# Half-width products of a head pair in two groups, and the softmax denominators and row of ones around them, in a two-layer attention kernel

## The reference, cut to what matters

```python
# per family: q, k (768 tokens), v
s = einsum('bqkgd,blkd->bkgql', qblk, k).astype(float32) * scale
p = softmax(s, axis=-1)
o = einsum('bkgql,blkd->bqkgd', p, v)
# latents read all 768 keys; context tokens read the 256 context keys (layer 0 only)
# gqa: 6 heads of 64; diff: 4 x 2 maps of 32, o1 - lam * o2, then rms_norm; mla: 6 heads of 64+32
y = concat(o * silu(g)) @ w_out
x = layer_norm(alpha * x + gate * y)
```

## Time and profile before

| | us |
|---|---|
| three runs, lowest, median, highest | 1100.06, 1102.35, 1105.29 |
| the profiled execution | 1105.77 |
| its span in the trace | 1103.9 |
| attention of layer 0 on PE, first max tile to last turned output | about 265 to 514 |
| attention of layer 1 | about 811 to 1031 |

### The profile page before, as it was taken

The page is one execution under the profiler, slowest core; times in us unless marked ns, Lnnn a source line. Parts: engine busy times, 40 slices in busy tenths (PEclk is TensorE's granted clock), DMA queues, the critical chain, the costliest instruction groups (busy, mean ns, idle before and its releaser), DMA issues.

```text
span 1103.9 us, 13093 instructions
## 1 busy us (share of the span) xinstructions
PE 969.0 (88%) x4607; PEld 684.6 (62%) x4607; DVE 594.0 (54%) x901; ACT 403.4 (37%) x815; POOL 524.8 (48%) x421
## 2 busy tenths in 40 slices
PE   4799999996899899998995299899968999999793
PEld 2478777985554455555784289789755445555572
DVE  5419230244568499824069548341645758782337
ACT  1521122314354466554200333133434445555320
POOL 2227232352557455553345337243626756566464
PEclk9799999996899899999998689899959989899997
DMA  9756451215232100012431022123142130001421
GB/s 364 270 178 218 157 188 40 77 31 125 55 77 65 34 16 8 16 58 79 169 96 77 38 62 72 58 65 85 49 101 65 37 72 16 15 16 58 160 69 77
DMA packets 44976, 96.91 MB, mean 88 GB/s; under 512 B 9592, under 2 KB 16656, under 8 KB 42864
## 3 DMA queue, kind: packets, MB, share of 16 engines
q1 hardware_dynamic: 43472, 90.83, 26.8%
q10 hardware_dynamic: 1440, 5.24, 1.2%
HBM read 71.33 MB, written 5.26 MB: 69 GB/s over the span
## 4 chain that ended last, share of the span: by engine, by line
PE 71%; DVE 10%; POOL 4%; ACT 4%; SPq 4%; DMA 3%; issue 3%; POOLq 0%; ACTq 0%; DVEq 0%
PE banks L762 13%; PE banks L764 12%; PE banks L763 12%; PE banks L936 11%; PE banks L956 9%; PE banks L914 5%; SPq L588 3%; PE banks L773 2%; DMA area_g<-in_w_ada_dram 2%; DVE negmax L1635 1%; PE banks L975 1%; DVE stats L1515 1%; DVE area_b L1779 1%; PE banks L968 1%; PE banks L826 1%
## 5 line engine op out<-in xcount | busy, mean ns | idle before, releaser
L1393 POOL TENSOR_TENSOR w_split<-w_raw,w_split 128x512 fp32r<-128x512 f32 (+4 forms) x124 | 146.2, 1184 | 258.7 <-ACT w_split L1138 258.6
L762 PE MATMUL banks<-w_split,area_a 128*128 128x512 f32 (+3 forms) x624 | 232.7, 373 | 16.4 <-DVE area_a L1845 9.9
L764 PE MATMUL banks<-w_split,area_a 128*128 128x512 f32 (+3 forms) x624 | 229.8, 368 | 0.0
L763 PE MATMUL banks<-w_split,area_a 128*128 128x512 f32 (+3 forms) x624 | 229.7, 368 | 0.0
L1635 DVE TENSOR_REDUCE negmax<-banks 128x1 f32<-128x768 f32 x160 | 149.6, 951 | 67.3 <-PE banks L914 66.4
L1138 ACT ACTIVATE w_split<-w_raw 128x512 fp32r<-128x512 f32 (+4 forms) x124 | 69.9, 581 | 278.1 <-PE banks L764 278.1
L936 PE MATMUL banks<-area_a 97*128 97x512 f32 (+4 forms) x448 | 135.7, 416 | 17.5 <-DMA area_a<-m_row 11.5
L762 PEld LDWEIGHTS banks<-w_split,area_a 128*128 128x128 f32 x624 | 119.4, 191 | 46.2 <-issue 16.4
L1237 ACT ACTIVATE area_z<-banks 128x512 f32<-128x512 f32 x196 | 109.1, 595 | 103.5 <-PE banks L936 98.2
L764 PEld LDWEIGHTS banks<-w_split,area_a 128*128 128x128 f32 x624 | 118.9, 190 | 16.6
L763 PEld LDWEIGHTS banks<-w_split,area_a 128*128 128x128 f32 x624 | 119.2, 191 | 15.5
(11 more groups left out here) (184 smaller groups left out, 1458.4 us busy)
## 6 DMA issues: line engine op xcount, KB each, us to landing
area_g<-in_w_ada_dram SPq DMA_DIRECT2D x16, 1024.0 KB, 5.8
w_raw<-in_w_in_dram SPq DMA_DIRECT2D x32, 512.0 KB, 3.7
area_g<-in_w_ada_dram SPq DMA_DIRECT2D x16, 512.0 KB, 5.0
w_raw<-in_w_out_dram SPq DMA_DIRECT2D x16, 512.0 KB, 3.9
area_a<-parts SPq DMA_DIRECT2D x72, 96.0 KB
area_a<-parts SPq DMA_DIRECT2D x30, 192.0 KB, 3.6
area_b<-in_x_dram SPq DMA_DIRECT2D x8, 512.0 KB, 9.8
x_mid<-area_b ACTq DMA_DIRECT2D x6, 512.0 KB, 2.7
```

The costliest lines, as they stand in the source:

```text
L762: nc.tensor.matmul(dst, a[0], b[0], start=first, stop=False)
L763: nc.tensor.matmul(dst, a[0], b[1], start=False, stop=False)
L764: return nc.tensor.matmul(dst, a[1], b[0], start=False, stop=last)
L1393: op = nc.gpsimd.tensor_tensor(lo, raw, hi.bitcast(F32), ALU.subtract)
```

## The change

The order of an attention layer is rewritten; the arithmetic stays.

- The step "ctx" comes first in a pair and not last, and its denominators are computed within the pair. The latent denominators of pair p-1 and the context ones of pair p share one bank and one copy.
- The mixes of a pair stand in two groups. After the scores of steps ctx, 0 and 1 come the last two mixes of the pair before (4 and 5), the context mix, the denominators, and mixes 0 and 1, with nothing between; after the scores of 2 and 3 come mixes 2 and 3 and the turned denominators.
- The maximum tiles are dealt out by a table, `max_counts`: how many stand at each of eleven places of a pair. c[3] is the place right ahead of the first group, c[4] the one behind it.
- The rows of ones are written once per layer into all eight blocks by eight DMAs (`load_ones`), behind the max row of pair 1; a diff unit then has six DMAs and not seven. SP loads unit 12 and 13 one pair later (the list with 12, 13 and 14 at p = 4), behind the max row of pair 4.
- `mla_high` of a pair's first head moves from the next pair to the end of its own, and ACT's copy of the latents stands ahead of the exponentials of step 1. On DVE `output_rows` comes after five to seven of the pair's tiles. Context output has buffers of its own.

The core of the diff (lines taken away are left out; they stand in the functions above):

```diff
+def max_counts(L, p):
+
+    if L < DEPTH - 1:
+        return {0: [1, 2, 0, 1, 2, 1, 1, 1, 0, 1, 3], 1: [1, 1, 2, 2, 1, 1, 0, 1, 1, 1, 0]}.get(p, [1, 1, 1, 1, 1, 1, 0, 1, 1, 1, 0])
+    return {0: [1, 0, 1, 1, 2, 1, 1, 0, 1, 1, 2], 1: [2, 1, 1, 1, 1, 1, 0, 1, 1, 1, 0]}.get(p, [1, 0, 1, 1, 1, 1, 0, 1, 1, 1, 0])
+
+
...
+            RING += [("s", _L, _p, s, u) for s in (("ctx", 0, 1) if ctx else (0, 1)) for u in range(2)]
+        if now and ctx:
+            RING += [("x", _L, _p)]
+        if last or ctx:
+            RING += [("d", _L, _p)]
+        if last and _p + 1 < NPAIR:
+            RING += [("rows", _L, _p + 1)]
         if now:
+            RING += [("s", _L, _p, s, u) for s in (2, 3) for u in range(2)]
         if head_pair(_p + 3):
             RING += [("mla", _L, 2 * _p + 6, part) for part in mla_parts(_L)]
+        if last or ctx:
+            RING += [("dt", _L, _p)]
+        if last:
...
+        if now:
+            RING += [("s", _L, _p, 5, u) for u in range(2)]
...
 N_CTX = count([(L, p) for L, p in PAIRS if L < DEPTH - 1])
 N_POOL_SUM = count([(L, p, s, u) for L, p in PAIRS for s in range(1, 5) for u in range(2)])
 N_DVE_SUM = count([(L, p, u) for L, p in PAIRS for u in range(2)])
+LOADS = {u: {"gqa": 3, "diff": 6, "mla": 3 if u in (16, 19) else 2}[family(u)] for u in range(NUNIT)}
...
+            def load_ones():
+
+                for b in range(1, 2 * KD, 2):
+                    move(blocks[96:97, b, :].rearrange("o (t n) -> o t n", n=P), across(ones_r[:], TILES)).then_inc(ones_in, 16)
...
                 for p in range(-1, NPAIR):
+                    for u in {-1: (2, 3), 0: (4, 5), 1: (6, 7), 2: (8, 9), 3: (10, 11), 4: (12, 13, 14), 5: (15, 16),
+                              6: (17,), 7: (18, 19)}.get(p, ()):
                         load_unit(L, u)
                     if p + 1 < NPAIR:
                         load_maxrow(L, p + 1)
+                    if p == 0:
+                        load_ones()
                     if p == 8:
+                        sp.wait_ge(ring_filled, N_RINGB["d", L, 4])
...
+                for p in range(NPAIR + 1):
+                    c = max_counts(L, p)
+                    now = p < NPAIR
+                    if now and context:
+                        scores(L, p, "ctx")
+                    maxima(c[0])
+                    if now:
+                        scores(L, p, 0)
+                    maxima(c[1])
+                    if now:
+                        scores(L, p, 1)
+                    maxima(c[2] + c[3])
+                    if p:
                         mix(L, p - 1, 4)
                         mix(L, p - 1, 5)
+                    if now and context:
+                        mix(L, p, "ctx")
+                    if p or context:
+                        denominators(L, p)
+                    if now:
+                        mix(L, p, 0)
+                        mix(L, p, 1)
+                    if p:
+                        turn_max(L, p + 1)
+                    maxima(c[4])
+                    if now:
+                        scores(L, p, 2)
+                    maxima(c[5])
+                    if now:
+                        scores(L, p, 3)
+                    maxima(c[6])
                     if head_pair(p + 3):
                         mla_head(L, 2 * p + 6)
+                    if now:
+                        mix(L, p, 2)
+                        mix(L, p, 3)
+                    if p or context:
+                        turn_denominators(L, p)
+                    maxima(c[7])
+                    if p:
+                        turn_output(L, p - 1)
+                    maxima(c[8])
+                    if now:
+                        scores(L, p, 4)
+                    maxima(c[9])
+                    if p == 0:
+                        turn_max(L, 1)
                     if head_pair(p + 3):
                         mla_head(L, 2 * p + 7)
+                    if now:
+                        scores(L, p, 5)
+                    maxima(c[10])
...
+                for p in range(NPAIR + 1):
+                    now = p < NPAIR
+                    if now and context:
+                        exponent(L, p, "ctx")
+                    if now:
+                        exponent(L, p, 0)
+                    if p:
                         copy_latents(L, p - 1)
+                    if now:
+                        exponent(L, p, 1)
+                    if p == 0:
+                        split_block(L, 4)
+                    if now and context:
+                        copy_context(L, p)
+                    if p or context:
+                        copy_denominators(L, p)
+                    if p:
+                        copy_maxrow(L, p + 1)
+                    if now:
+                        exponent(L, p, 2)
                     if head_pair(p + 2):
                         mla_high(L, 2 * p + 5)
+                    if now:
+                        exponent(L, p, 3)
                     if head_pair(p + 3):
                         mla_copy(L, 2 * p + 6)
+                    if now:
+                        exponent(L, p, 4)
+                    if p == 0:
+                        copy_maxrow(L, 1)
+                        split_block(L, 6)
+                    if head_pair(p + 3):
+                        mla_copy(L, 2 * p + 7)
+                    if now:
+                        exponent(L, p, 5)
                     if (L, p - 1) in N_NORMED:
                         squares(L, p - 1)
                     if p == 2:
                         split_block(L, 10)
+                    if head_pair(p + 3):
+                        mla_high(L, 2 * p + 6)
...
                 for p in range(NPAIR + 1):
+                    if (L, p - 2) in N_NORMED:
+                        gate(L, p - 2)
                     if p == 0:
                         split_block(L, 4)
                     if p < NPAIR:
+                        sum_probs(L, p, 1)
                         sum_probs(L, p, 2)
+                        sum_probs(L, p, 3)
+                    if p and (L, p - 1) not in N_NORMED:
                         gate(L, p - 1)
+                    if p == 0:
+                        split_block(L, 6)
                     if p < NPAIR:
                         sum_probs(L, p, 4)
+                    if (L, p - 1) in N_NORMED:
                         diff_root(L, p - 1)
                     if p == 2:
...
+                    if p:
+                        sum_last(L, p - 1, 0)
+                        sum_last(L, p - 1, 1)
+                    if (L, p - 2) in N_NORMED:
+                        diff_norm(L, p - 2)
                     if head_pair(p + 2):
                         mla_low(L, 2 * p + 4)
+                    maxima(c[2] + c[3] + c[4])
+                    if p == 2:
+                        gain_gates(L)
+                    maxima(c[5] + c[6])
                     if head_pair(p + 2):
                         mla_low(L, 2 * p + 5)
+                    if p or context:
+                        reciprocals(L, p)
+                    maxima(c[7])
+                    if p:
+                        output_rows(L, p - 1)
+                    if (L, p - 1) in N_NORMED:
+                        diff_combine(L, p - 1)
+                    maxima(c[8])
                     if head_pair(p + 3):
                         mla_rope(L, 2 * p + 6)
+                    maxima(c[9] + c[10])
                     if head_pair(p + 3):
                         mla_rope(L, 2 * p + 7)
...
```

More of the change, by code:

```diff
@@ L258 @@
             RING += [("mla", _L, 2 * _p + 7, part) for part in mla_parts(_L)]
-        if now and ctx:
-            RING += [("s", _L, _p, "ctx", u) for u in range(2)]
+        if now:
+            RING += [("s", _L, _p, 5, u) for u in range(2)]
 N_RINGB = count(RING)
@@ L264 @@
 N_O = count([r for r in RING if r[0] == "o"])
+N_D = count([r for r in RING if r[0] == "d"])
 N_RING_FREE = count([r for r in RING if r[0] == "mla"])
@@ L1025, in attend, with maxima @@
-                max_tile(L, 2, 4)
-                max_tile(L, 2, 5)
-                for p in range(1, NPAIR):
-                    scores(L, p, 0)
-                    max_tile(L, p + 1, 6)
-                    scores(L, p, 1)
-                    max_tile(L, p + 1, 7)
-                    if context:
-                        mix(L, p - 1, "ctx")
-                    else:
+                tiles = iter([(p, i) for p in range(NPAIR) for i in range(len(max_tiles(L)))])
+                def maxima(n):
+                    for p, i in itertools.islice(tiles, n):
+                        max_tile(L, p, i)
```

266 lines of the change are left out of this document (70 added, 196 removed).

## The result

| | before | changed |
|---|---|---|
| median of four runs, us | 1101.20 | 1156.25 |
| lowest and highest | 1099.50 to 1105.29 | 1149.48 to 1158.47 |
| ratio of the runs, 95% interval | | 1.0484 [1.0429, 1.0539] |
| profiled execution, its span | 1105.77, 1103.9 | 1149.48, 1147.6 |

The change costs 55 us where 25 were forecast, and the time lies above the range. The ratio is estimated from all the runs and is not the quotient of the medians (1.0500). The profiled execution of the changed kernel is the fastest of its four, with a mean granted clock of 0.910 against 0.897 to 0.904 in the others, and that of the kernel before (1105.77) is slower than all four of its runs above, so the two traces show 43.7 us of span and not 55.

What follows compares the result with a forecast made beforehand. PE, busy for 88% of the span, was taken to bound the kernel, in its two attention stages. Costs of 66.2 us less gains of 41.6 gave +24.6, taking the median from 1102.35 to 1127; range 1084 to 1146.

Steps and rivals of the forecast that it cites:

- a: Pair 1, both layers: eight ones DMAs on SP's queue delay unit 6; 7.1 us lost, between 0 and 14.
- e: The denominators' bank stands behind two more copies on ACT: 0.3 us in nine pairs, 2.7 lost.
- the old waits: PE's waits for `m_row` ahead of pair 4 (5.8 us), `gain_gates` (2.0) and exponentials (5.7), expected to go.
- f: Attention stages: slow clock behind the new waits, two stretches at 3.3 us, 6.6 lost, bounds 0 and 23.
- the old stretch: Slow clock behind the 3.67 us wait for `m_row` ahead of pair 4; 3.3 us expected to be gained.
- gain 1: PE's mixes in both layers: 80 fewer groups at 0.35 us, less 3.2 lost to mode changes, 24.8 gained.
- the clock falls behind every new wait: Seven waits over 3 us slow the clock, costing 23 us and not 6.6: 1144; part of the slower case, 0.72.
- d: Pairs 5 to 7: the tile ahead of the group waits for `mla_low`; 20.8 us lost in layer 0, 9.0 in layer 1.
- c: Pair 3: PE's tile waits for unit 10, made late by a chain through `gain_gates`; 10.7 us in layer 0, 4.8 in layer 1.
- b: `turn_max` of pair 1 waits about 1.5 us in each layer, 3.0 lost; unit 8 in pair 2 late, 1.5 lost.
- Gain 2: Ahead of pair 4: `m_row` waits and slow clock go as two loads move a pair later; 9.1 us gained, bounds 5.8 and 9.1.
- The faster rival: The tile ahead of the group isn't late, so c and d leave 3 us: 1078; chance 0.18.

Runs made afterwards that it cites:

- e8: The changed kernel with four added 512-column products on PE ahead of the tile in pairs 5 to 7 of layer 0; 1144.84 us, ratio 1.0389.
- e5: The kernel before with only mixes 0 and 1, and mixes 2 and 3, joined on PE; 1101.93 us, ratio 1.0020.
- e12: The changed kernel with the four products of `gain_gates` dealt out over pairs 1 and 2, two in each; 1151.11 us, ratio 1.0424.
- e11: The changed kernel with the rows of ones loaded with each diff unit, as before; 1151.01 us, ratio 1.0433.
- e6: The kernel before with only SP's list of the change, units 12 and 13 loaded a pair later; 1100.05 us, ratio 0.9974.
- e1: The changed kernel with one tile per pair moved behind the first group in layer 0, pairs 1 to 9; 1126.05 us, ratio 1.0226.
- e13: The changed kernel with tile behind group, `mla_high` behind step 0, gain products dealt out, and latents copy, another tile and DVE's sums later; 1116.23 us, ratio 1.0143.

## Why the prediction was wrong

The direction was right, and so was the place of most of the loss. For both layers together, against the two profiled traces:

| us | forecast | measured |
|---|---|---|
| idling: costs a to e less the old waits (59.6 - 13.5) | +46.1 | +38.9 |
| slow clock: f less the old stretch (6.6 - 3.3) | +3.3 | +14.4 |
| groups: gain 1 | -24.8 | -11.7 |
| sum | +24.6 | +41.6 |

The remaining 2.1 us of the 43.7 lie outside the two stretches, and the 11 between 43.7 and 55 lie in executions that have no trace but a lower mean clock. So two terms were mis-sized, by 11 and 13 us, and the idling came out 7 us lower.

- **The first step that failed is f, "Slow clock behind the new waits".** I took two stretches of 3.3 us, with a bound of seven waits over 3 us. The clock fell behind waits of 1.35 and 2.8 us too (pairs 2 and 5), so six of the pairs 1 to 7 have a slow stretch. With the 3.4 that went (half of the 6.8 us at half clock behind the wait for `m_row`), the new stretches cost 18.4 us in layer 0, within the bound of 23 and far from 6.6. The rival "the clock falls behind every new wait" was nearer, but the clock doesn't fall behind every wait: the kernel before has longer ones than 1.35 us with no slow stretch behind them. Its 1144 was still too little, since it kept gain 1 as it was. e8 shows the cause, as far as the group behind the wait goes. The Trainium skill, "TensorE: Matmul & The Clock Gate", section "HAM oscillation — how this bites in real kernels", describes a kernel in which each wait for a transfer makes the next burst start at the low clock; the traces of the change agree in layer 0, and show it behind a wait of 1.35 us too; the traces of the kernel before have waits of 2.47 and 2.17 us without it.
- **The second is gain 1, the groups.** 0.35 a group was read rightly from the rows of one pair, but e5 gives 0.23 and 0.29 of PE's time a group, and in the change what is left of PE's busy time fell by 5.5 us in layer 0 and by 6.2 in layer 1, where 14.2 and 10.6 were forecast. The count was off as well: the trace of before has 57 and 46 groups of mixes and not 66 and 56, which come out only if the denominators that stood alone, nine in each layer, are counted with them (55 in layer 1 even then). So 61 groups of mixes went and not 80. What took the rest of the gain isn't shown; e5 turned none of it into time.
- **d, pairs 5 to 7, was right in mechanism and size:** forecast 7.4, 7.0 and 4.8; measured 2.76 + 3.71, 2.76 + 3.71 and 1.51 + 3.54, so 6.5, 6.5 and 5.1. The ACT block of squares and `mla_high` shows as the first of each pair of numbers, DVE's chain as the second. Layer 1: forecast 9.0, measured 7.7.
- **c, unit 10:** forecast 10.7 and 4.8, measured 5.36 and 3.32. The chain was drawn through `gain_gates`; in the trace ACT's half of the split came last, 1.08 us behind it, and e12 shows that the wait stays when `gain_gates` is dealt out.
- **a and b:** of the 5.3 us for the rows of ones 1.5 came, of the 1.8 in layer 1 1.6, and e11 shows that loading them with the units is no better. Unit 8 was late by 1.35, as forecast (1.5). Pair 1 didn't wait for its `m_row`.
- **Not foreseen** in layer 0: 2.8 us in pair 1 for a tile behind DVE's sums, seven waits of 0.3 to 0.8 for `output_rows` (3.9), and e's 0.3 was nearer 0.5.
- **Gain 2:** the two waits of `m_row` went as forecast, and e6 gives them 3 us of time and not 9.
- **The faster rival** ("the tile ahead of the group isn't late") fell at once; its mend, e1, gives 1126 and not 1078, since late inputs were not the only cost.

Not settled: e13 is still 16 us slower than the kernel before, with fewer groups. It idles 7 us more in layer 0 and 8 more in layer 1, and its slow clock costs 6.3 more in layer 0 and 1.0 less in layer 1; with the busy time that it saves, the two profiled executions differ by 8.6 us of span. Whether the context's place at the head of a pair forces that was not tried by itself.

## What to carry to other kernels

Where PE is the busiest engine, a wait costs its length, and it may cost a slow stretch behind it. In layer 0 here the slow clock added about half of the idling again, in layer 1 nothing; so count the waits of over one us that a new order brings, and carry their slow clock as a range from nothing to two thirds of the idling. An instruction that may have to wait belongs behind the long run of work that needs nothing from it, not in front: that was the one edit that gave back half of the loss. And a price read from a few rows of one pair is to be tried by itself before it is multiplied by 80.

## What the runs showed of the hardware

Idling PE can be worth filling: four products of 512 columns put into a wait of 3.7 us shortened the slow stretch from 10.2 to 3.4 us, and the group behind took 1.76 and not 3.47 us, while it started 0.2 us later.

The gain products on DVE read two operands from SBUF, and POOL's sums do so too. One product takes 0.55 us where it begins ahead of POOL's sum, and up to 1.64 where it begins beside one. Here are a product of the changed kernel and the sum that it began beside, then a product of e12 and its sum:

```profile
345.42 1.64 DVE L1714 TENSOR_TENSOR area_g<-area_g,sgain 128x384 f32<-128x384 f32 x1
```

```profile
345.28 1.36 POOL L1431 TENSOR_TENSOR w_raw<-w_raw,area_z 128x512 f32<-128x512 f32 x1 [2.24 <-ACT area_z L1241]
```

```profile
344.54 0.77 DVE L1714 TENSOR_TENSOR area_g<-area_g,sgain 128x384 f32<-128x384 f32 x1
```

```profile
343.54 1.35 POOL L1431 TENSOR_TENSOR w_raw<-w_raw,area_z 128x512 f32<-128x512 f32 x1 [2.24 <-ACT area_z L1241]
```

The first product ends at 347.06, 0.42 us behind the end of POOL's sum (346.64), the second at 345.31, again 0.42 behind the end of POOL's (344.89): DVE's instruction got on only when POOL's was over. That agrees with the rule of the Trainium skill, "SBUF — State Buffer", section "Who interferes with whom", that the prediction quoted.
